# Doubling levels of a chunked delta rule on half of the columns, packed in PSUM

## The reference

```
decay = exp(where(causal, gc_i - gc_j, -inf))
m     = where(strict, (k*beta) @ k.T * decay, 0)      # strictly lower
sol   = triangular_solve(m + I, rhs, unit_diagonal=True)
u, w  = sol[..., :dv], sol[..., dv:]
# per chunk: v_new = u - w @ S;  o = q*exp(g) @ S + qk @ v_new;  S = S*exp(g_last) + k.T @ v_new
```

## Time and profile before

| | us |
|---|---|
| median of 3 runs (3168.75 to 3175.38) | 3171.87 |
| span of the profiled execution | 3168.8 |
| stage `delta_prompt`, from its first matmul to its last DVE work | 1488.8 to 1762 |
| levels 1 to 6 of the four pairs, T of level 1 to the state read | 38 to 39 each |

### The profile page before, as it was taken

How to read it: one execution, slowest core, us unless ns; L and a number is a source line. 1 busy time by engine, 2 the same in 40 slices (tenths; PEclk the granted TensorE clock), 3 DMA queues, 4 the chain that set the end, 5 groups by cost and what they waited for, 6 DMA issues and landing times. The chain is left out here.

```text
span 3168.8 us, 44503 instructions
## 1 busy us (share of the span) xinstructions
PE 2852.2 (90%) x17430; PEld 2588.8 (82%) x17444; DVE 1479.7 (47%) x2283; ACT 901.8 (28%) x1419; POOL 199.2 (6%) x373
## 2 busy tenths in 40 slices
PE   7999999999869999777888488889789999999997
PEld 6999999999768799653788355459589999999995
DVE  3232233223545678548888576451422322333336
ACT  2111111111233567602455344341331111111113
POOL 0000000000000000122000000660000000000000
PEclk8999999999989999859999699899999999999999
DMA  3111111110031122333000200873021111111101
GB/s 119 41 43 49 48 40 46 40 46 26 19 97 41 48 77 75 111 79 97 27 28 8 95 1 1 226 205 108 14 67 41 44 44 48 41 48 41 41 21 57
DMA packets 264695, 185.66 MB, mean 59 GB/s; under 512 B 61711, under 2 KB 244191, under 8 KB 264518
## 3 DMA queue, kind: packets, MB, share of 16 engines
q1 hardware_dynamic: 213190, 113.51, 12.6%
q0 software_dynamic: 20640, 58.46, 5.5%
q10 hardware_dynamic: 30688, 11.27, 1.4%
HBM read 156.96 MB, written 26.22 MB: 58 GB/s over the span
## 5 line engine op out<-in xcount | busy, mean ns | idle before, releaser
L351 DVE TENSOR_TENSOR ffn_hidden<-ffn_hidden,ffn_ps_b 128x1092 f32<-128x1092 f32 x44 | 56.9, 1292 | 398.2 <-PE ffn_ps_b L85 398.2
L309 ACT ACTIVATE ffn_h_hi<-ffn_hidden 128x1092 fp32r<-128x1092 f32 x44 | 49.3, 1121 | 494.7 <-DVE ffn_hidden L351 494.7
L294 ACT ACTIVATE ffn_hi_d<-ffn_raw_d 128x1024 fp32r<-128x1024 f32 x40 | 42.4, 1061 | 494.7 <-PE ffn_ps_b L85 379.2
L85 PE MATMUL ffn_ps_a<-mixer_mix_hi,ffn_hi_g 128*128 128x364 f32 x528 | 117.5, 330 | 23.6 <-DVE ffn_lo_g L334 19.4
L302 ACT ACTIVATE ffn_hidden<-ffn_ps_a 128x1092 f32<-128x1092 f32 x44 | 47.8, 1085 | 287.0 <-PE ffn_ps_a L85 287.0
L85 PE MATMUL ffn_ps_a<-first_x_hi,ffn_hi_g 128*128 128x364 f32 x528 | 117.1, 330 | 5.9 <-DVE ffn_lo_g L334 5.9
L196 POOL DMA_DIRECT2D ffn_raw_d<-in_ffn_w_down x40 | 21.3, 532 | 1580.5 <-DVE ffn_lo_d L340 1394.7
L85 PE MATMUL ffn_ps_a<-first_x_lo,ffn_hi_g 128*128 128x364 f32 x528 | 117.2, 330 | 0.0
L85 PE MATMUL ffn_ps_a<-mixer_mix_lo,ffn_hi_g 128*128 128x364 f32 x528 | 117.1, 330 | 0.0
L85 PE MATMUL ffn_ps_a<-first_x_hi,ffn_lo_g 128*128 128x364 f32 x528 | 116.4, 329 | 0.0
L85 PE MATMUL ffn_ps_a<-mixer_mix_hi,ffn_lo_g 128*128 128x364 f32 x528 | 116.3, 329 | 0.0
(11 more groups left out here) (603 smaller groups left out, 6914.3 us busy)
## 6 DMA issues: line engine op xcount, KB each, us to landing
ffn_raw_d<-in_ffn_w_down POOLq DMA_DIRECT2D x40, 512.0 KB, 3.7
proj_raw<-in_w_in SPq DMA_DIRECT2D x22, 512.0 KB, 3.8
second_ffn_raw_g<-in_ffn_w_gate SPq DMA_DIRECT2D x22, 512.0 KB, 3.6
second_ffn_raw_u<-in_ffn_w_up SPq DMA_DIRECT2D x22, 512.0 KB, 5.0
first_ffn_raw_g<-in_ffn_w_gate SPq DMA_DIRECT2D x21, 512.0 KB, 3.7
first_ffn_raw_u<-in_ffn_w_up SPq DMA_DIRECT2D x21, 512.0 KB
scratch_qkv<-proj_stage POOLq DMA_DIRECT2D x12, 544.0 KB, 3.0
delta_cur<-scratch_qkv SPq DMA_DIRECT2D x8, 768.0 KB, 5.5
```

What stands on the lines that cost most here:

```text
L85: last = pe.matmul(out[:, s, 0:USED[s]], w(k), x(k)[:, s * SL:s * SL + USED[s]], start=start and n == 0 and p == 0, stop=stop and n == len ...
L294: act.activation(d_hi[:, k, :], raw["d"][:, :], ACT.Copy).then_inc(whi_done["d"], 1)
L309: act.activation(h_hi[:, par, fb, :], act_buf[:, fb, :], ACT.Copy).then_inc(hhi_done, 1)
L351: dve.tensor_tensor(hid, hid, ps_b[:, :, 0:SL], ALU.mult).then_inc(mul_done, 1)
```

## The change

At level l only the columns of odd blocks of T, of U and of `tt` can be nonzero, and only the columns of even blocks of XB and of `ml`. The changed kernel streams only those 64 of 128 columns through PE, writes the results of the four heads next to each other in the first 256 columns of a PSUM bank, and lets ACT and DVE read that packed half and touch only the matching columns of `tt`, Y, X and `ml`. The stationary operands stay 128 by 128. Level 0 stays whole. Since the mask no longer writes the other half of `ml`, POOL clears `ml` once at the start of the stage; DVE clears `tt` once. Columns of `tt` that a former level left give rows of XB that do not belong to the level; X is updated with one instruction that multiplies XB by a column of -1 and 0 per row (`odd_rows`, made once from the masks) and adds X.

```diff
+def halves(v, l, odd):
+    return v.rearrange("p h (n a c) -> p (h n) a c", a=2, c=1 << l)[:, :, odd, :]
+def half_of_head(v, l, odd):
+    return v.rearrange("p (n a c) -> p n a c", a=2, c=1 << l)[:, :, odd, :]
+def packed(bank, l):
+    return bank.rearrange("p h v -> p (h v)")[:, 0:GH * P // 2].rearrange("p (n c) -> p n c", c=1 << l)
+def packed_head(bank, h, l):
+    return packed(bank, l)[:, h * (P // 2 >> l):(h + 1) * (P // 2 >> l), :]
...
+            for g in range(2):
+                pool.memset(ml[:, g], 0.0).then_inc(s["masks_cleared"], 1)
...
-                        last = pe.matmul(t_bank[g][:, h, :], ml[:, g, l, h, :], y[:, c % 4, h, :],
-                                         start=True, stop=True)
+                        last = pe.matmul(packed_head(t_bank[g], h, l), ml[:, g, l, h, :],
+                                         half_of_head(y[:, c % 4, h, :], l, 1), start=True, stop=True)
...
-                        last = pe.matmul(u_bank[g][:, h, :], x[:, g, h, :], tt[:, g, h, :], start=True, stop=True)
+                        last = pe.matmul(packed_head(u_bank[g], h, l), x[:, g, h, :],
+                                         half_of_head(tt[:, g, h, :], l, 1), start=True, stop=True)
                         if l < LEVELS - 1:
-                            last = pe.matmul(x_bank[g][:, h, :], tt[:, g, h, :], x[:, g, h, :], start=True, stop=True)
+                            last = pe.matmul(packed_head(x_bank[g], h, l), tt[:, g, h, :],
+                                             half_of_head(x[:, g, h, :], l, 0), start=True, stop=True)
...
+                    if l == 1 and p == 0:
+                        act.wait_ge(s["tt_cleared"], 1)
...
-                        act.activation(tt[:, g], t_bank[g][:, :, :], ACT.Copy).then_inc(s[f"t_copied{g}"], 1)
+                        act.activation(halves(tt[:, g], l, 1), packed(t_bank[g], l), ACT.Copy
+                                       ).then_inc(s[f"t_copied{g}"], 1)
...
+                if c < 2 and l == 0:
+                    dve.wait_ge(s["masks_cleared"], 2)
...
+                shape = [P, GH, P // 2 >> l, 1 << l]
+                mask = half_of_head(levels[l], l, 0).unsqueeze(1).to_broadcast(shape)
+                dve.tensor_tensor(halves(ml[:, g, l], l, 0).rearrange("p (h n) c -> p h n c", h=GH),
+                                  halves(m[:, g], l, 0).rearrange("p (h n) c -> p h n c", h=GH), mask, ALU.mult
                                   ).then_inc(s[f"level_made{g}"], 1)
...
-                dve.tensor_tensor(y[:, c % 4], y[:, c % 4], u_bank[g][:, :, :], ALU.subtract).then_inc(s[f"y_upd{g}"], 1)
+                yh, xh = halves(y[:, c % 4], l, 1), halves(x[:, g], l, 0)
+                dve.tensor_tensor(yh, yh, packed(u_bank[g], l), ALU.subtract).then_inc(s[f"y_upd{g}"], 1)
                 if l < LEVELS - 1:
-                    dve.tensor_tensor(x[:, g], x[:, g], x_bank[g][:, :, :], ALU.subtract).then_inc(s[f"x_upd{g}"], 1)
+                    dve.scalar_tensor_tensor(xh, packed(x_bank[g], l), odd_rows[:, l:l + 1], xh, ALU.mult, ALU.add
+                                             ).then_inc(s[f"x_upd{g}"], 1)
...
+            dve.memset(tt[:, :, :, :], 0.0).then_inc(s["tt_cleared"], 1)
+            for l in range(1, LEVELS - 1):
+                ins = dve.tensor_reduce(odd_rows[:, l:l + 1], levels[l], AX.X, ALU.max)
+            own(ins)
+            own(dve.tensor_scalar(odd_rows[:, 1:LEVELS - 1], odd_rows[:, 1:LEVELS - 1], -1.0, None, ALU.mult))
```

More of the change, by code:

```diff
@@ L1178, in delta_prompt @@
         ml = sc.sb("ml", [P, 2, LEVELS, GH, P])
+        odd_rows = sc.sb("odd_rows", [P, LEVELS])
         sums, exps = sc.sb("sums", [P, 3, n_chunks, GH]), sc.sb("exps", [P, 3, n_chunks, GH])
@@ L1459, in level_mask @@
                         dve.wait_ge(s[f"t_done{g}"], 6 * (c // 2))
-                dve.tensor_tensor(ml[:, g, l], m[:, g], over_heads(levels[l]), ALU.mult
+                if c < 2 and l == 0:
+                    dve.wait_ge(s["masks_cleared"], 2)
+                if l == 0:
+                    dve.tensor_tensor(ml[:, g, l], m[:, g], over_heads(levels[l]), ALU.mult
+                                      ).then_inc(s[f"level_made{g}"], 1)
+                    return
+                shape = [P, GH, P // 2 >> l, 1 << l]
+                mask = half_of_head(levels[l], l, 0).unsqueeze(1).to_broadcast(shape)
+                dve.tensor_tensor(halves(ml[:, g, l], l, 0).rearrange("p (h n) c -> p h n c", h=GH),
+                                  halves(m[:, g], l, 0).rearrange("p (h n) c -> p h n c", h=GH), mask, ALU.mult
                                   ).then_inc(s[f"level_made{g}"], 1)
```

## The result

The changed kernel takes 3213.07 us (median of 4 runs, 3205.29 to 3219.21) against 3170.31 of the kernel before in the same session (4 runs, 3167.24 to 3175.38): a ratio of 1.0135, 95% interval 1.0115 to 1.0154. The forecast was 3243 us, 3195 to 3280, slower with a chance of 0.85.

The account below looks back on a forecast made before the run. It took PE's passes, plus subtractions T(0) does not cover, to bound a level. Halving would save no PE time but leave the clock low: +47 to +95, middle +71, on 3171.87 gives 3243 us, range 3195 to 3280.

Parts of the forecast that it names:

- A pass of 64 columns is not shorter: PE passes of U, T and XB: 0.110 to 0.112 us with 64 columns against 0.112 with 128; counted 0.
- The levels start at 0.50 and stay there: PE clock in the four pairs' levels: begins at 1.2 GHz after the wait and stays; +94 us if nothing raises it.
- rival 2: Levels run at 2.4 GHz throughout, decided by the clock when T of level 1 starts; -14 us, 3158; chance 0.09.
- the 59.6 of the sum: Last pair's levels at 1.2 GHz: 5 x 10.5 + 7.1 = 59.6 us instead of 38.0, +21.6.
- Whether the sums of gates raise it: Gate sums after levels 2 and 3 of the first three pairs may raise the clock: +8 a pair instead of +24.
- The lower form: Slow case in which gate sums raise the clock in the first three pairs: +47 us, 3219.
- the half slow level: Allowance of +3 us in each of the first three pairs, within the +8, if gate sums raise the clock.
- Around the levels, +1: State reads at low clock +4 us together, less 3 for level 1's half masks and DVE's shorter last update.
- The head, +1: Stage head: DVE's memset and six small instructions, partly hidden by its wait, +1 us (0 to +2.6); POOL's memsets 0 to +4.
- The sum of +47 to +95: All terms of the slow case, from gate sums raising the clock to nothing raising it; chance 0.85.
- The middle of two forms, +71: Middle of +47 and +95, taken because no row was known to tell the ends apart; gives 3243 us.

Follow-up runs that it names:

- (C): Changed kernel with POOL's clearing of `ml` held back until DVE has made the sums, behind the scaling of `odd_rows`; 3215.32 us (one run).
- both cures: Changed kernel with level 1 streaming 128 columns and the head's seven new DVE instructions moved behind the first search step; 3153.68 us, ratio 0.9938 to the kernel before.
- the first experiment: Changed kernel with T, U and XB of level 1 streaming 128 columns again, levels 2 to 6 still 64; 3156.35 us, ratio 0.9956 to the kernel before.

## Why the prediction was right, point by point

1. *A pass of 64 columns is not shorter.* Right, and shown: 32 passes in 3.57 us with 64 columns and with 128, at the same clock.
2. *The levels start at 0.50 and stay there.* They stay there; the start was misread. In the kernel before, too, T of level 1 of the second pair began at 1.00 and the clock fell under it, and the row at 1576 us is already behind the fall:

```profile
1574.00:1575.50 1.50, 1.16 (x8) 0.96 (x8) 1.50 (x3) 1.50 (x4) 0.55 (x1) 1.00 0.00 0
```

   In the changed kernel pairs 2 to 4 did the same. So the granted clock when T of level 1 starts, the one row that was to decide for rival 2, read 1.00 in three pairs, and the levels were slow all the same: that row does not decide. The last pair took 57.7 us for the 59.6 of the sum, since T's 16 passes go in 3.41 us from start to start (1736.34 to the first U at 1739.75), where the row of before, with its first waits in it, gave 3.67, and since level 1 had its first 1.5 us at 1.00. With 128 columns in level 1 this cost is gone (34.0 us).
3. *Whether the sums of gates raise it.* The lower form came: in the first three pairs of this profile, each time behind level 2. The term was +8 a pair and measured +5.4, +4.4 and +4.3; the half slow level allowed for was not needed here, but in (C) two pairs paid a whole one, 6 us more. So this term is itself a range from run to run, some 4 to 11 us a pair.
4. *Around the levels, +1.* Measured -2.7: the clock was up again at the first three state reads, and T of level 1 waits 1.14 us for its mask instead of 1.41.
5. *The head, +1, at most +2.6 from DVE.* Wrong in size and bound: +4.6, of it 2.9 from DVE and 1.6 from the clock at the products of keys and queries, for which the forecast had no term. (The sum of +47 to +95 leaves out the head's +1: it is 46 + 1 and 94 + 1, and that 1 is the work around the levels.) For DVE's part the step that failed is that each small instruction was taken to cost between nothing and 0.48 us, by a memset that ran with POOL idle; one stood 2.78 us beside POOL's clearing, which I had priced only as a wait for the first mask.
6. *The middle of two forms, +71.* Measured: +35.6 in the stage and +42.8 between the medians; the lower form was +47. (Between +35.6 and +42.8 lie the 3.6 us outside the stage and the spread of the runs.) So 3213 lies below the centre of 3243 and inside the range because the range held both forms; that the lower one came is no merit of the forecast. I wrote that no row tells the two apart. There was one that leaned, in the head of the stage before, where four passes of 512 columns over 128 rows stood at 0.50 and the clock rose with them. It would not have settled it: in the kernel with all levels at 128 columns the same four passes left the clock at 0.50. Windows of the kernel before, then of that kernel (the four passes, and the transposes behind them):

```profile
1488.90:1493.50 4.60, 4.55 (x8) 1.94 (x8) 3.25 (x7) 0.28 (x1) 0.00 (x0) 0.50 0.74 192
1493.80:1498.00 4.20, 2.72 (x23) 2.52 (x24) 3.78 (x6) 2.12 (x2) 0.00 (x0) 1.00 0.74 170
```

```profile
1495.50:1499.20 3.70, 3.70 (x5) 1.11 (x5) 3.50 (x8) 0.00 (x0) 3.70 (x2) 0.50 0.90 229
1501.00:1506.00 5.00, 4.98 (x24) 4.98 (x24) 4.93 (x9) 2.26 (x3) 0.00 (x0) 0.50 0.27 64
```

7. *Rival 2's price.* With the clock up the halved DVE work gives 4 us a pair rather than the 3 I had (3.0, 5.0, 5.1, 4.0 in the kernel with level 1 at 128 columns): in pairs 2 and 3 the clock also stays at 1.00 there, where before it fell for some 3 us in each. The wait ahead of T of level 1 is not the reason: it is 1.14 or 1.15 us there, as in the changed kernel, where the clock fell each time. That 128 columns behind the wait hold it is not shown either, since with both cures it fell in pair 3, behind the same 1.14 us.

## What to carry to other kernels

Before halving what a matmul streams, look in the trace for a pass with fewer columns against weights of the same size: where it is no shorter, nothing is saved, and PE may be left at its low clock behind the next wait. Halve what the other engines read instead, and keep the wide streams at least in the first work behind a wait: in all twelve pairs of the three kernels here that did so, the clock was 1.00 before level 1 ended. Price a new instruction by a row in which the engines beside it do what they will do there.

## What the runs showed of the hardware

- Passes of 64 columns against 128 by 128 weights ran at a clock of 1.00 without a fall (levels 2 to 6 of the last pair of the first experiment, 27 us) and left one of 0.50 where it is (55.8 us in the changed kernel, 64.7 in the one with the sums in pieces, PE busy throughout). Right behind the wait between pairs the clock fell from 1.00 to 0.50 under them, in all three pairs of the changed kernel that began at 1.00.
- The two passes of a 512-column sum raise it in some places and not in others: behind level 2 three times of three in the changed kernel and once of three in (C). Added before level 1, the sum raised it in pair 1; in the other three pairs the clock was 1.00 up to the sum, and fell with it in two.
- A tensor_scalar of 128x5 from SBUF to SBUF took 2.78 us beside a POOL memset and ended 0.02 us behind it; two tensor_tensor of 128x512 with both inputs in SBUF took 1.29 us beside it, as in the kernel before with POOL idle. The Trainium skill has this in "SBUF — State Buffer", section "SBUF: two separate sides": DVE's modes that use both ports and GpSimd share one pair of ports by an exclusive lock, and an operation with two SBUF inputs meets it only against a GpSimd operation that reads SBUF. These rows agree; in which of its modes DVE ran the scaling, no row shows.
